# MLP up products in seven block products for eight, with r squared applied in the additions after the down products

## What is computed

```python
def _rmsnorm(x, g):
    xf = x.astype(jnp.float32)
    y = xf * lax.rsqrt(jnp.mean(xf * xf, axis=-1, keepdims=True) + EPS)
    return (y * g.astype(jnp.float32)).astype(x.dtype)

def _sqrelu_mlp(h, w1, w2):          # w1: 1024 x 4096, w2: 4096 x 1024
    u = jax.nn.relu(h @ w1)
    return (u * u) @ w2
...
    for i in range(DEPTH_2):         # DEPTH_2 = 2: retention, then chunk attention
        hn = _rmsnorm(h, mix_norm_g[i])
        ...
        h = h + _sqrelu_mlp(_rmsnorm(h, mlp_norm_g[i]), mlp_w1[i], mlp_w2[i])
    return _rmsnorm(h, final_norm_g)
```

## Time and profile before

| | before |
|---|---|
| median of 3 runs | 1957.34 us (1957.2 to 1957.37) |
| the profiled execution | 1958.46 us |
| its span | 1956.7 us |
| PE busy | 1938.3 us (99%), 9216 matmuls |
| DVE busy | 1205.2 us (62%) |
| ACT busy | 880.1 us (45%) |
| POOL busy | 603.0 us (31%) |

### The profile page before, as it was taken

The page is one execution under the profiler, slowest core; times in us unless marked ns, Lnnn a source line. Parts: engine busy times, 40 slices in busy tenths (PEclk is TensorE's granted clock), DMA queues, the critical chain, the costliest instruction groups (busy, mean ns, idle before and its releaser), DMA issues.

```text
span 1956.7 us, 23662 instructions
## 1 busy us (share of the span) xinstructions
PE 1938.3 (99%) x9216; PEld 1609.5 (82%) x9216; DVE 1205.2 (62%) x1701; ACT 880.1 (45%) x1284; POOL 603.0 (31%) x442
## 2 busy tenths in 40 slices
...
PEclk9999999999999999999999999999999999999999
...
GB/s 164 94 44 76 97 98 116 93 123 112 94 86 87 119 76 94 79 87 85 86 86 151 128 173 179 123 172 129 107 86 85 86 65 183 173 128 172 122 179 86
DMA packets 166338, 221.31 MB, mean 113 GB/s; under 512 B 4640, under 2 KB 120096, under 8 KB 166112
## 3 DMA queue, kind: packets, MB, share of 16 engines
...
## 4 chain that ended last, share of the span: by engine, by line
PE 89%; DVE 4%; ACT 2%; issue 2%; POOL 1%; DMA 1%; SPq 0%; DVEq 0%; ACTq 0%; POOLq 0%
PE ps L925 28%; PE ps L927 28%; PE ps L926 28%; PE ps L1097 1%; PE ps L1127 1%; POOL w_lo L819 1%; PE ps L1136 1%; PE ps L1137 1%; PE ps L1114 1%; DVE scr L2601 1%; DMA aux<-in_mlp_w 0%; PE ps L1467 0%; ACT w_hi L1612 0%; ACT w_hi L1630 0%; DVE w_lo L3011 0%
## 5 line engine op out<-in xcount | busy, mean ns | idle before, releaser
L819 POOL TENSOR_TENSOR w_lo<-raw,w_hi 128x512 fp32r<-128x512 f32 x376 | 529.8, 1440 | 667.4 <-ACT w_hi L1612 667.4
L925 PE MATMUL ps<-hn_hi,w_hi 128*128 128x512 f32 x1524 | 602.4, 395 | 2.2 <-DVE hn_lo L2710 1.7
L927 PE MATMUL ps<-hn_hi,w_lo 128*128 128x512 f32 x1524 | 593.8, 390 | 0.0
L926 PE MATMUL ps<-hn_lo,w_hi 128*128 128x512 f32 x1524 | 593.7, 390 | 0.0
L925 PEld LDWEIGHTS ps<-hn_hi,w_hi 128*128 128x128 f32 x1524 | 286.4, 188 | 66.3 <-issue 4.1
L927 PEld LDWEIGHTS ps<-hn_hi,w_lo 128*128 128x128 f32 x1524 | 286.2, 188 | 60.6
L926 PEld LDWEIGHTS ps<-hn_lo,w_hi 128*128 128x128 f32 x1524 | 286.5, 188 | 58.9 <-issue 1.7
L1612 ACT ACTIVATE w_hi<-raw 128x2048 fp32r<-128x2048 f32 (+1 forms) x98 | 186.0, 1898 | 286.9 <-PE ps L927 286.8
L1630 ACT ACTIVATE w_hi<-raw 128x1024 fp32r<-128x1024 f32 x112 | 116.1, 1056 | 205.2 <-PE ps L927 205.0
L925 PE MATMUL ps<-w_hi,hid_hi 128*128 128x512 f32 x456 | 177.7, 390 | 0.2
L926 PE MATMUL ps<-w_lo,hid_hi 128*128 128x512 f32 x456 | 177.4, 389 | 0.0
...
## 6 DMA issues: line engine op xcount, KB each, us to landing
raw<-in_mlp_w SPq DMA_DIRECT2D x56, 1024.0 KB, 5.4
raw<-in_ret_w_in SPq DMA_DIRECT2D x24, 1024.0 KB, 5.2
aux<-in_mlp_w POOLq DMA_DIRECT2D x16, 1024.0 KB, 8.9
raw<-in_att_w_in SPq DMA_DIRECT2D x12, 1024.0 KB, 5.5
raw<-in_w_gate SPq DMA_DIRECT2D x11, 1024.0 KB, 5.4
raw<-in_w_up SPq DMA_DIRECT2D x11, 1024.0 KB, 5.3
raw<-in_w_down SPq DMA_DIRECT2D x8, 1024.0 KB, 8.0
raw<-in_ret_w_out SPq DMA_DIRECT2D x8, 1024.0 KB, 5.0
```

What stands on the lines that cost most here:

```text
L819: ins = pool.tensor_tensor(w_lo[:, slot, at], raw[:, slot, at], w_hi[:, slot, at].bitcast(F32), ALU.subtract)
L925: pe.matmul(o, hi, rhs_hi, start=start, stop=False, skip_group_check=True)
L926: pe.matmul(o, hi, rhs_lo, start=False, stop=False, skip_group_check=True)
L927: return pe.matmul(o, lo, rhs_hi, start=False, stop=stop, skip_group_check=True)
```

## The change

A group's 1024 features now go in two *units* of 512. A unit's product (512 x 1024 by 1024 x 512) is itself done in seven block products for eight (`unit_up`, order of `UNIT_PRODUCTS`: A11, A12, S3, M, A21, S4, S1), each of 2 x 4 x 3 = 24 matmuls of 128x256. Group 0 of each MLP keeps two of the old up products (`plain_up`) for its first 512 features, and has one unit; groups 1 to 3 have two: seven units in an MLP, fourteen in the program.

- The weight operands S3 and S1 of a unit come from accumulating DMAs on POOL within SBUF (`unit_sums`: chain += A22, then A22 += A21, 128x1024 float32 each, 512 KB, one after the other); M and S4 are made from the chain on DVE (`unit_m_sum`, `unit_s4_sum`, 128x1024 each). The chain's first block comes by a load of its own (`load_chain`).
- The activation operands T3, T2, T4, T1 of the normed x are made once for each MLP: ACT scales four pieces of x (`gained_b12`), DVE makes the sums (`first_sums`, 12 instructions of 128x256 with the gain as a scalar, and one of 128x1024), ACT and DVE the high and low parts (`first_t`).
- The result blocks of a unit: ACT copies four from PSUM (`kept`, 128x2x256), DVE adds to them (`c00`, `c10`, `c11_c01`, four instructions of 128x2x256), ACT then does relu and the square (`squared`, two instructions of 128x1024 each; before, relu was on DVE).
- r is no longer in the relu. As relu(r u)^2 = r^2 relu(u)^2, each `take` now multiplies by r^2 (`r_two`, a scalar for each token) as it adds: two instructions of 128x512 where one of 128x1024 stood. The sum over partitions for r is four matmuls with one column (`stat_columns`) instead of two of 512.
- All eight sets of transposes now lie among the products of plain up 1, and PE waits for all eight token copies before the first unit.
- Parts and sums of the down stage (`part_hi`, `part_lo`, `t3`, `t2`, `t4`, `t1`) go as one instruction of 128x1024 where two of 128x512 stood.
- Halves of slots are counted by *places*; one number (HOLE, 11) is left out in group 0, so that what follows it falls on the other half.

The core of the diff:

```diff
@@ PE
+            UNIT_PRODUCTS = ((Mlp.U_A11, B11, 0, True), (Mlp.U_A12, B21, 1, True), (Mlp.U_S3, T3, 2, True),
+                             (Mlp.U_M, T2, 1, False), (Mlp.U_A21, T4, 2, False), (Mlp.U_S4, B12, 0, True),
+                             (Mlp.U_S1, T1, 1, False))
+            def unit_up(ml, norm, g, u):
+                for n, block, which, opens in UNIT_PRODUCTS:
...
+                    pe.wait_ge(s["w_lo_ready"], ml.ready(place))
...
+                    for m in range(2):
+                        at = slice(m * P, m * P + P)
+                        for k in range(4):
+                            ins = three(ps[:, bank, 256 * m:256 * m + 256], hi[:, k, at], lo[:, k, at],
+                                        x_hi[:, k, :], x_lo[:, k, :], opens and m == 0 and k == 0, m == 1 and k == 3)
...
                 for g in range(MLP_GROUPS):
-                    for m in range(4):
-                        mlp_up(ml, g, m, normed(norm) if (g, m) == (0, 0) else None,
-                               {(0, 1): in_second, (0, 2): in_third}.get((g, m)))
+                    if g == 0:
+                        plain_up(ml, 0, normed(norm))
+                        plain_up(ml, 1, None, in_second)
+                        pe.wait_ge(s["x_copied"], kept + KD)
+                    else:
+                        unit_up(ml, norm, g, 0)
+                    unit_up(ml, norm, g, 1)
@@ POOL
+            def unit_sums(ml, g, u):
+                pool.wait_ge(s["chain_in"], ml.chains_landed(g))
...
+                pool.dma_start(chains[u], a22, accum_op=ALU.add).then_inc(s["s3_added"], 16)
+                pool.wait_ge(s["s3_added"], ml.summed(g, u))
+                pool.dma_start(a22, a21, accum_op=ALU.add).then_inc(s["s1_added"], 16)
+                pool.wait_ge(s["s1_added"], ml.summed(g, u))
@@ SP
+                    if g + 1 < MLP_GROUPS:
+                        load_raw(g + 1, 0, w1[g + 1, 0], KD)
+                        sp.wait_ge(s["group_done"], ml.done(ml.down(g, ml.M, 1)))
+                        for u in range(2):
+                            load_chain(g + 1, u)
+                        load_raw(g + 1, 1, w1[g + 1, 1], KD)
+                        sp.wait_ge(s["group_done"], ml.done(ml.down(g, ml.S1, 1)))
+                        for n in range(2):
+                            load_pair(g + 1, n)
@@ ACT
+                def squared(g, u, t):
+                    rows = u_squared[:, 4 * u:4 * u + 4, 256 * t:256 * t + 256]
+                    act.wait_ge(s["up_read"], ml.unit_step(g, u, (ml.C10, ml.C01)[t]))
+                    act.activation(rows, rows, ACT.Relu).then_inc(s["mlp_up_taken"], 1)
+                    act.wait_ge(s["mlp_up_taken"], ml.ups(g, u, (ml.RELU_0, ml.RELU_1)[t]))
+                    act.activation(rows, rows, ACT.Square).then_inc(s["mlp_sq"], 1)
@@ DVE
+                def t3(g):
+                    dve.wait_ge(s["mlp_sq"], ml.squared(g, 1, 1))
+                    dve.tensor_tensor(p_block(T3), p_block(T3), p_block(B12), ALU.subtract).then_inc(s["mlp_sum"], 1)
```

811 lines of the change are left out of this document (535 added, 276 removed).

## The result

The changed kernel takes 2023.61 us (median of 4 runs, 2022.75 to 2025.75) against 1957.36 before: 66 us more, a ratio of 1.0339 with an interval of 1.0326 to 1.0351. The forecast was slower, 1981.2, with 1998 as the longest time of any case. The direction is right and the size is not: 66 us where 24 were forecast. The profiled execution took 2023.56 us with a span of 2021.6.

A forecast was written before the change was run, and what follows sets the result against it. It took PE alone, busy 99%, to bound the kernel. Its terms, -22.8 + 11.4 + 16.2 + 11.2 + 4.3 + 3.6 = +23.9 us, gave a median of 1981.2 us, with a range of 1955 to 1996.

The forecast's parts named there:

- PE's work: Matmuls over the whole program: fourteen cheaper units and narrower sums for r give PE less to do, -22.8 us.
- A: Start of each MLP: PE waits for the first token copy, 5.7 us each, +11.4 in all.
- B: Down stages of groups 1 to 3: PE waits for DVE, 2.7 us a group, +16.2 in all.
- C: Down stage of group 0: the left-out place delays t3; PE waits 5.6 us per MLP, +11.2 in all.
- D: Unit 0's weight sums, groups 1 to 3: accumulating DMA takes 7.0 us, PE waits 0.7 a group, +4.3 in all.
- Rival 2: Unit 0's weight sums: DMA fully crowded, 9 to 9.7 us, total 1994 to 1998 us; chance 0.13.
- E: PE's clock may fall to half during A's wait: 1.8 us for each MLP, +3.6 in all.
- DVE without idle time from t3 to Q5: Sign in the down stages: DVE never idles between these two while PE waits for it.
- by far more than 3: Sign against the forecast: it is wrong if S3 of unit 0 waits by far more than 3 us.
- PEclk under 1.00 only after A's wait: Sign for PE's clock: it falls only behind A's wait at each MLP's start, nowhere else.

The follow-up runs named there:

- e6: Changed kernel, SP holding unit_raw until unit 0's first sum landed and aux until unit 1's, with c00 of unit 0 ahead of DVE's Q3 additions; 1988.83 us.
- e1: Changed kernel with the token copies earlier in ACT's order at each MLP's start, copies 0 and 1 right behind the scaled copies; 2008.06 us.
- e5: Changed kernel with DVE's down-stage order edited: c11 and c01 ahead of A12's first low part, the Q5 additions ahead of Q4; 2015.03 us.
- e7: e1 with the left-out place moved from 11 to 4 and A12's high and low part behind T1's; 2007.06 us.
- e4: Changed kernel where SP issues unit_raw and S3's first block (3 MB) only when unit 0's first sum has landed; 2009.1 us.
- e8: Changed kernel with the edits of e1, e5 and e6 together; 1971.99 us.
- e9: e8 with unit 1's chain block loaded behind unit_raw, and c00, copy Y and copy Z moved earlier on DVE and ACT; 1961.15 us.

## Why the prediction was wrong

- **PE's work** (-22.8): right to 1 us. Matmuls of 128x256 are 0.1200 apart in the units too, and e6's up stage of 41.3 leaves no room for more. The one-column matmuls cost 0.8 in each MLP and not 0.5 for both; that no row shows one was an oversight, as the kernel before has four of them at 662.2 us, in eight rows 0.11 apart.
- **A** (5.7 in each MLP): right, 5.48 with 0.17 of restart. e1 shows it.
- **B** (2.7 a group, in four pieces before M, A21, S1 and S4): right, 2.5 in those places and 3.0 with the slower starts behind them. e5 shows the cause.
- **C** (5.6): right in size, 5.3 to 5.8. The cause by the place left out is shown by e7 for 2.0 of the 2.8 that it was to explain.
- **D** (0.7 a group, 4.3 in all): the step that failed. It took 5.4 us for the raw load and 7.0 for the sum. Measured 8.0 and 9.7, and some 5 us of waits a group at S3 and M. (By the prediction's own terms, 8.64 - 7.9 + 5.3 hides 6.04 us of the sum and not 6.2, so that 7.0 gives 5.8 in all; this is not what failed.) The 7.0 was worked out from 8.7 for 1 MB: the text named the three loads beside the sum and then took a value "nearer to the low end as the size is half". What decided was not the size but what ran beside it: the same 512 KB take 4.5 us alone (e4, e6) and 9.7 with 3 MB beside them. The bound of the sum, 9.7, was right, but it was put on a wrong start. The raw load itself stood behind 2 MB (the first piece and two chain blocks), and was priced by 5.4, the median of its kind. The kernel before shows how far such loads lie apart, in the view of L730:

```profile
DMA to landing us min/median/max: 4.9/5.4/10.6
```

Where e8 has the same 2 MB ahead of the raw piece, it lands after 7.6 to 8.7 us in the six groups; e9, with one chain block fewer ahead, has 6.1 to 7.2. Rival 2 had the length of the sum and not the start, and so ended at 1998.
- **E** (3.6 in all): the second failed step, in two ways. "The waits of B to D are below 2.8 each and cost none" fell with D: the waits at S3 and M were followed by 3.4 us at half clock in five of six groups and 6.8 in one. And the stretch behind A is 10 and 7 us long, not 3.6.

In numbers, by the two profiled executions: the spans differ by 64.9 us where the sum said 23.9, so 41 were missing. The six up stages of two units are 39.3 longer than PE's work in them, where D stood with 4.3: that is 35 of the 41, and e6 takes 32.8 of the 39.3 away. A's clock cost some 7 where 3.6 stood. The down stages, with 17.7 for B's six and 11.3 for C's two, are 1.6 above their terms, and the columns 1.1. The direction was forecast by terms that held, A, B and C, and the size missed by D. The waits cover one another (e1 gave back 15.6, e5 8.6, e6 34.8, 59.0 in sum, but e8 with all three gained 51.6), so single prices hold only with the others in place.

Of the prediction's own signs, DVE without idle time from t3 to Q5 came true, and S3 waited 3.4, not "by far more than 3"; "PEclk under 1.00 only after A's wait" did not: the trace has half clock at the turn to each of groups 1 to 3 of both MLPs.

The Trainium skill's price of a sum (DMA: Bandwidth & Descriptors, section Anatomy of one DMA — SWDGE (gpsimd) path), by its fit an estimate of 3.2 us, is nearer to the 4.5 alone than to the 9.7; the fit has a term for the size and none for what runs beside it. Its section Queues, rings and completion order says that each DMA engine takes turns between queues by packets, which fits a sum that becomes longer as loads run beside it; no run here shows the turns themselves.
